# Eight more projections in the seven-product scheme, and a new filling of the attention, in a decoder layer on one core

## The reference, cut to what matters

```
u = x @ w_in ; h = h + ... swiglu (first feed-forward)
proj = u @ w_in     -> gq gk gv gr ga dq dk dv gates   (gates: 2 x 1024 columns, gr: 4 x 128)
ya = gla(gq, gk, gv, ...)                              # linear attention, 4 heads
ya = rmsnorm(ya, gla_head_norm) * silu(gr)
yb = diff_attention(dq, dk, dv, ...)                   # 4 heads, two softmax maps each
yb = rmsnorm(yb, diff_head_norm) * (1 - lam_init)
g_a, g_b = sigmoid(gates)
h = h + gate * ((g_a * (ya @ w_branch_a) + g_b * (yb @ w_branch_b)) @ w_out)
... second feed-forward, final norm
```

## Time and profile before

| what | value |
| --- | --- |
| median of 3 runs | 2144.24 us |
| the profiled execution, its own time | 2143.3 us |
| its span | 2141.5 us |
| TensorE busy | 2106.8 us, 98% of the span, 10225 matmuls |
| VectorE, ScalarE, GpSimd busy | 1354.6, 841.9, 1349.1 us |
| mean granted clock of TensorE | 0.996 |

### The profile page before, as it was taken

The page is one execution under the profiler, slowest core; times in us unless marked ns, Lnnn a source line. Parts: engine busy times, 40 slices in busy tenths (PEclk is TensorE's granted clock), DMA queues, the critical chain, the costliest instruction groups (busy, mean ns, idle before and its releaser), DMA issues.

```text
span 2141.5 us, 28194 instructions
## 1 busy us (share of the span) xinstructions
PE 2106.8 (98%) x10225; PEld 1733.8 (81%) x10225; DVE 1354.6 (63%) x2077; ACT 841.9 (39%) x1571; POOL 1349.1 (63%) x1072
## 2 busy tenths in 40 slices
PE   8999999999999999999999999999999999999998
PEld 7788778778878788888788888888788888888887
DVE  6867777778956921288666663534766444459956
ACT  7432223234445433345444452114423332234444
POOL 6688878878964677543322132336688877769943
PEclk9999999999999999999999999999999999999999
DMA  7245555558333333300111013411243333366333
GB/s 286 86 142 170 177 163 162 182 189 296 90 100 112 119 99 109 88 11 2 40 40 30 21 40 122 165 49 49 84 151 97 111 101 118 104 225 202 94 99 123
DMA packets 228618, 248.86 MB, mean 116 GB/s; under 512 B 10479, under 2 KB 155010, under 8 KB 228226
## 3 DMA queue, kind: packets, MB, share of 16 engines
q1 hardware_dynamic: 228338, 246.81, 35.7%
q10 hardware_dynamic: 144, 0.26, 0.0%
HBM read 191.98 MB, written 55.05 MB: 115 GB/s over the span
## 4 chain that ended last, share of the span: by engine, by line
PE 77%; DVE 13%; DMA 4%; issue 3%; ACT 2%; SPq 1%; POOL 0%; DVEq 0%; ACTq 0%; POOLq 0%
PE ps L2883 27%; PE ps L3038 16%; PE ps L2758 15%; PE ps L2894 6%; PE ps L2839 5%; DMA ada_half<-in_w_ada 3%; PE ps L3290 2%; PE ps L3255 1%; DVE x_op L2248 1%; DVE ada_acc L2058 1%; DMA ada_full<-in_w_ada 1%; DMA q<-in_ffn_w_out 1%; PE ps L3171 1%; PE ps L3275 1%; PE ps L3104 1%
## 5 line engine op out<-in xcount | busy, mean ns | idle before, releaser
L1213 POOL TENSOR_TENSOR w_lo<-w_raw,w_hi 128x512 fp32r<-128x512 f32 x240 | 352.2, 1478 | 91.5 <-ACT w_hi L1506 90.7
L2883 PE MATMUL ps<-t,w_hi 128*128 128x512 f32 x1280 | 396.9, 391 | 7.0 <-POOL w_lo L1213 3.4
L3038 PE MATMUL ps<-x_op,w_hi 128*128 128x512 f32 x1208 | 373.5, 390 | 4.3 <-DVE x_op L2248 3.0
L1506 ACT ACTIVATE w_hi<-w_raw 128x512 fp32r<-128x512 f32 x240 | 143.3, 624 | 381.1 <-POOL w_raw L1278 168.5
L2883 PEld LDWEIGHTS ps<-t,w_hi 128*128 128x128 f32 x1280 | 240.0, 188 | 61.3 <-DVE bufs L2271 7.0
L3038 PEld LDWEIGHTS ps<-x_op,w_hi 128*128 128x128 f32 x1208 | 226.1, 188 | 54.9 <-POOL w_lo L1213 5.7
L1213 POOL TENSOR_TENSOR w_lo<-q,w_hi 128x512 fp32r<-128x512 f32 x132 | 198.2, 1511 | 102.2 <-ACT w_hi L1506 102.2
L2883 PE MATMUL ps<-t,w_lo 128*128 128x512 f32 x640 | 249.5, 390 | 0.0
L1180 POOL TENSOR_SCALAR w_hi<-w_raw 128x1024 fp32r<-128x1024 f32 x41 | 44.4, 1084 | 323.0 <-PE ps L2758 267.8
L3038 PE MATMUL ps<-x_op,w_lo 128*128 128x512 f32 x604 | 235.1, 389 | 0.0
L2248 DVE TENSOR_TENSOR x_op<-x_raw,x_op 128x512 fp32r<-128x512 f32 x154 | 177.8, 1164 | 83.8 <-ACT x_op L1516 82.7
(11 more groups left out here) (402 smaller groups left out, 4408.0 us busy)
## 6 DMA issues: line engine op xcount, KB each, us to landing
w_raw<-in_ffn_w_in SPq DMA_DIRECT2D x88, 512.0 KB, 4.0
hid_dram<-hid_raw SPq DMA_DIRECT2D x154, 256.0 KB, 5.1
x_raw<-hid_dram SPq DMA_DIRECT2D x154, 256.0 KB, 2.6
ada_half<-in_w_ada SPq DMA_DIRECT2D x112, 256.0 KB, 2.7
w_raw<-in_w_in SPq DMA_DIRECT2D x41, 512.0 KB, 3.7
q<-in_ffn_w_out SPq DMA_DIRECT2D x6, 1536.0 KB, 9.1
ada_full<-in_w_ada SPq DMA_DIRECT2D x16, 512.0 KB, 12.3
gate_dram<-h SPq DMA_DIRECT2D x12, 512.0 KB
```

What stands on the lines that cost most here:

```text
L1213: nc.gpsimd.tensor_tensor(lo, src, hi.bitcast(F32), ALU.subtract).then_inc(hs_ready, 1)
L1506: nc.scalar.activation(hs_place(n)[0], src, ACT.Copy).then_inc(wa_high, 1)
L2883: mm = nc.tensor.matmul(ps[bank][:], w[i], x[:, k, :], start=(first and k == 0 and q == 0), stop=(k == 3 and q == 2), skip_group_check=True)
L3038: mm = nc.tensor.matmul(ps[down_bank(p) + m][:], w[:, tile(m)], x_op[:, n % 3, x, :], start=(p in (0, 1, 3) and k == 0 and q == 0), stop=( ...
```

## The change

**More in the seven-product scheme.** `GATES` grows from 12 to 20 units: all 16 gate units and the four r units (`C_GR`), so `gate_tile` runs 11 times instead of 7. For the r tiles ScalarE applies Silu instead of sigmoid. r comes back from `gate_dram` to `r_row` four times, at the start of the attention, and GpSimd multiplies `ya` by it (`gate_r`, 8 instructions). The gain of the norm moves into `norm_a` of VectorE (`scalar_tensor_tensor` for `tensor_tensor`).

**Filling by quarters.** Heads 0 to 2 have six half units (q, k, v, v, q, k) for eight steps. Each is cut in quarters of 6 matmuls and every step gets three quarters, 18 matmuls, some of them ahead of `key_scores` and some behind:

```diff
+        HALF_UNITS = [("q", 0), ("k", 0), ("v", 0), ("v", 1), ("q", 1), ("k", 1)]
+        BEFORE_SCORES = {1: (0, 3, 4), 2: (1, 2, 4), 5: (3, 3, 4), 6: (4, 2, 4)}
+        BEHIND_SCORES = {0: (0, 0, 3), 1: (1, 0, 2), 2: (2, 0, 1), 3: (2, 1, 4),
+                         4: (3, 0, 3), 5: (4, 0, 2), 6: (5, 0, 1), 7: (5, 1, 4)}
```

(step: half unit, first quarter, last quarter). In TensorE's order:

```diff
                         turn_a(hd, i)
                         if i == 1 and hd > 0:
                             turn_out(hd - 1, 1)
-                        if i == 6:
-                            fill(hd, i)
+                        if hd + 1 < DIFF_H and i in BEFORE_SCORES:
+                            fill(hd, BEFORE_SCORES[i])
...
-                        if i != 6:
-                            fill(hd, i, (lambda: turn_v_half(0, 0)) if (hd, i) == (0, 0) else None)
+                        if hd == DIFF_H - 1:
+                            filled(i)
+                        elif i != 6:
+                            fill(hd, BEHIND_SCORES[i], (lambda: turn_v_half(0, 0)) if (hd, i) == (0, 0) else None)
...
                         values(hd, i)
+                        if i == 6 and hd + 1 < DIFF_H:
+                            fill(hd, BEHIND_SCORES[i])
```

**The last head** is filled by `filled(i)`: one token half of a row of the first branch, 12 matmuls a step, four rows in all. For this the parts of `ya` must be there: ScalarE makes the high parts in head 2, step 4 and head 3, step 0 (four copies of 128x512 each, `high_ya`), GpSimd the low parts (`low_ya`, eight instructions), and GpSimd gates the eight finished pieces (`gate_row`):

```diff
+            def filled(i):
+                m, hf = filled_row(i)
+                if i == 0:
+                    pe.wait_ge(dqlo, 4 * DIFF_H)
+                else:
+                    pe.wait_ge(row_kept, i)
...
+                for k in range(4):
+                    if m == 0:
+                        pe.wait_ge(ylo_ready, 4 * hf + k + 1)
+                    mm = row_three(0, m, k, hf, ps[0])
```

**ScalarE's order.** The copy out of bank 0 is in steps 1, 2, 5 and 6 of heads 0 to 2 right behind `high_a`, in 3 and 7 behind `exps`; in the last head in every step behind `exps`:

```diff
-                        if i == 6:
+                        if hd < DIFF_H - 1 and i in BEFORE_SCORES:
                             fill_out(hd, i)
...
+                        if (hd, i) == (DIFF_H - 2, 4):
+                            high_ya(0)
+                        if (hd, i) == (DIFF_H - 1, 0):
+                            high_ya(1)
-                        if i != 6:
+                        if hd == DIFF_H - 1 or i in (3, 7):
                             fill_out(hd, i)
```

**VectorE's order.** `combine` is done one step ahead instead of two, ahead of `maxima`:

```diff
                         ahead = (hd, i + 2) if i + 2 < TT else (hd + 1, i + 2 - TT)
+                        following = (hd, i + 1) if i + 1 < TT else (hd + 1, 0)
+                        if following[0] < DIFF_H:
+                            combine(*following)
                         if ahead[0] < DIFF_H:
                             maxima(*ahead)
...
-                        if ahead[0] < DIFF_H:
-                            combine(*ahead)
```

More of the change, by code:

```diff
@@ L49 @@
 U_GA, U_GQ, U_GK, U_GV = 0, 1, 3, 5
-U_HEAD, U_BRANCH = 9, 25
-U_OUT = U_BRANCH + 12
+U_HEAD, U_BRANCH = 9, 21
+U_OUT = U_BRANCH + KT
 MIX_UNITS = U_OUT + KT
[L53 to L56, removed]
+FILLED = 4
+BRANCH_UNIT = {(br, i): U_BRANCH + 4 * br + i for br in range(2) for i in range(4)}
 MB = 0
-GATES = [(0, m) for m in range(EARLY + 1, KT)] + [(1, m) for m in range(KT)]
+GATES = [(br, m) for br in range(2) for m in range(KT)] + [(2, hd) for hd in range(GLA_H)]
+SIGMOID_TILES = KT
 GATE_TILES = len(GATES) // 2
@@ L274, in build_program, with y_part @@
         ratio = sm("ratio", [P, 2])
[L276 to L283, removed]
+        def y_part(br, part, j, hf=None):
+            if br == 0:
+                return u_hi[:, hf, 4 * part + j, :]
+            row = ((0, 1, 4, 6), (2, 3, 5, 7))[part][j]
+            if hf is None:
+                return rar[:, row * S:(row + 1) * S]
+            return rar[:, row * S + hf * HALF:row * S + (hf + 1) * HALF]
         z = [far[:, j * S:(j + 1) * S] for j in (6, 7, 5, 8, 0, 1, 2, 3)]
@@ L1840, in exps, with high_ya, high_yb @@
                                              accum_out=lsum[:, i % 2, m:m + 1]).then_inc(exp_ready, 1)
-                def high_y(br, j):
-                    copy(y_hi[br][j], (ya if br == 0 else yb)[:, j, :], yhi_ready)
+                def high_ya(hf):
+                    act.wait_ge(rt_ready, 2 * DIFF_H)
+                    for j in range(4):
+                        copy(y_part(0, 0, j, hf), ya[:, j, half(hf)], yhi_ready)
+                def high_yb(j):
+                    copy(y_part(1, 0, j), yb[:, j, :], yhi_ready)
                 def high_a(hd, i):
@@ L2613, in mixer @@
                 dve.wait_ge(bias_ready, 3)
-                for i in range(2):
-                    maxima(0, i)
-                    combine(0, i)
+                maxima(0, 0)
+                combine(0, 0)
+                maxima(0, 1)
                 for hd in range(DIFF_H):
@@ L2662, in mixer @@
                 for br in range(2):
-                    for m in range(KT):
+                    for m in range(0 if br else FILLED, KT):
                         if br == 0 and m >= 4:
-                            low_y(1, m - 4)
+                            low_yb(m - 4)
                         if (br, m) == (1, 6):
```

386 lines of the change are left out of this document (192 added, 194 removed).

## The result

| | before | after |
| --- | --- | --- |
| median | 2144.14 us (4 runs, 2140.76 to 2148.03) | **2177.07 us** (4 runs, 2173.47 to 2178.80) |
| the profiled execution, its span | 2143.3, 2141.5 | 2178.8, 2177.1 |
| mean granted clock of TensorE | 0.996 | 0.993 |

The ratio of the times is 1.0151, with a 95% interval of 1.0131 to 1.0170. The kernel became slower by 1.5%, about 33 us. The forecast was slower by 1.0%, 2165.6 us, with a range of 2135 to 2179: the direction and the range hold, and 11.5 us are missing from the sum. The time lies above the forecast's own range of 2153 to 2175, by 2 us, and inside the one that belonged to rival 3.

The account below looks back on a forecast made before the run. TensorE bounds the kernel, by a hair over the VectorE-ScalarE loop. 2143.3 - 10.9 (matmuls) + 15.9 (heads 0 to 2) + 14.4 (last head) + 2 (GpSimd) = 2164.7; median 0.9 higher: 2165.6 us, range 2135 to 2179.

Parts of the forecast that it names:

- the forecast's own range: Whole kernel: 2153 to 2175 us, for waits of 20 to 40 us in the attention; chance 0.48.
- rival 3: Attention: some nine waits over 1 us each bring 1.6 us at 1.2 GHz, +14, 2180 us; chance 0.13.
- Work by place: TensorE's matmuls: tile stage +76.2 us, attention -54.4, behind it -32.6; 48 matmuls fewer, -10.9 in all.
- The waits: Attention: TensorE waits for the VectorE and ScalarE loop, +5.3 us in each of heads 0 to 2, +14.4 in the last.
- the walk: Attention, instruction by instruction with measured durations: +5.3 us a head in heads 0 to 2; last head ends at 59.8.
- The clock, taken at 0: TensorE's clock: no drop counted in the sum, as waits stand between dense fills; 0 us.
- Head 2 was counted like the others: Attention, heads 0 to 2: the same +5.3 us for each, +15.9 for three.
- rival 3's "against": Attention: at a lower clock TensorE fills part of a wait that it would have had.
- the +2 for GpSimd: Last head: VectorE's combines slowed by 16 more GpSimd instructions, +2 us; +14 if all are hit, 0 if none.
- Rival 1: Attention: only TensorE's work counts, the loop overlaps better; faster, 2133.3 us; chance 0.24.
- rival 2: Attention: heads 0 to 2 hide their lag, only the last head waits; 2148 us, no change; chance 0.13.
- Rival 4: Tile stage: 23 us a tile, 11 x 4 us more than the sum, 2200 us; chance 0.02.

Follow-up runs that it names:

- Run 9: Changed kernel with each of ScalarE's 32 squares in the attention done twice; 2190.6 us, ratio 1.0216 to the kernel before.
- run 1: Changed kernel with VectorE's old order, combine(i+2) behind maxima(i+2); 2169.5 us, ratio 1.0103 to the kernel before.
- run 7: Run 1's kernel with the next key and query parts ahead of exps(7) and combine(7), and high_ya(0) moved to step 6 of head 2; 2163.9 us.
- run 8: Run 7's kernel, last head from step 2: ScalarE does squares, copy, next high part, then exps; VectorE combines i+1 behind maxima(i+2); 2161.7 us.
- run 11: Run 8's kernel with the second halves of the fifth and sixth half rows exchanged in the last head, copy never put off; 2154.4 us.
- run 10: Changed kernel with GpSimd's last-head work cut: 8 columns instead of 512 per gated row, 8 of 1024 in two weight splits; 2171.8 us, ratio 1.0128.
- run 6: Changed kernel with 240 extra matmuls filling all attention heads, 54.4 us of TensorE's work; 2193.0 us, ratio 1.0222 to the kernel before.

## Why the prediction was right, and where it fell short

- **Work by place.** -10.9 us in matmuls, +76.2, -54.4 and -32.6 by stage: confirmed, to 0.1 us in the tile stage and behind the attention; in the attention the work went, but not the time.
- **The range.** The forecast's own part of it, 2153 to 2175, missed. The stated range of 2135 to 2179 holds the measured 2177.1 because it took in half of rival 3. By the profiled executions 14.1 us are missing (2178.8 against 2164.7): 10.7 in the attention, 259.0 against 248.3 (270.4 - 54.4 + 32.3), and 3.8 ahead of the tile stage, less 0.3 in the linear attention.
- **The waits.** Forecast 5.3 us in each of heads 0 to 2 and 14.4 in the last; measured idle 6.2, 5.4, 6.4 and 13.6. By place they differ. Step 4 waited 0.71 for the copy (forecast 0.9), step 5 0.62 (1.3), step 6 0.59 for the key's low part and 0.72 for `low_a` (1.5 and 1.1). Two that the walk had at 0.2 or not at all made up for it: 1.45 at `turn_out` in step 1 and 1.06 for `keep_b` in step 6, which stands behind `maxima(7)` on VectorE. The sums agree, and this agreement is partly luck. Run 9 and runs 1, 7, 8 and 11 show that the mechanism is the right one.
- **The clock, taken at 0.** The reason given was "My sum has no such drop, since the waits here stand between dense fills", and it failed. Counted over the whole kernel, as the time that 128x512 matmuls took above 0.227 us where they start at the low pace, it is 10.2 us after against 4.7 before, 5.5 more. All of it is in head 2 and the last. One stretch of the last head, 1352 to 1360, had a clock of 0.57:

```profile
1352.00:1360.00 8.00, 6.18 (x18) 5.02 (x19) 2.73 (x5) 3.52 (x10) 1.28 (x1) 0.57 0.00 0
```

  In it and just ahead of it lie the idle 1.98 and 1.84 us of step 6. The Trainium skill ("TensorE: Matmul & The Clock Gate", Part 1) says that only activity keeps the array off half rate. The trace agrees, with 0.57 here. No run shows which waits draw a drop. Rival 3 was right in kind and at 14 us too high: the waits of heads 0 and 1 drew no drop. The 5.5 us are not all lost time either: by run 10 the drop of head 2, about 1.5 of them, cost nothing, as rival 3's "against" has it. In the last head no two runs separate the clock from the waits. In the filled run 6 the same count is 3.1 us.
- **Head 2 was counted like the others.** This step failed: it carries `high_ya(0)`, 2.17 us ahead of `high_a(5)` and the copy; I had only `high_ya(1)` of the last head. Its length was 2.5 above head 1's. In run 7, with `high_ya(0)` in step 6 and `combine` two ahead, heads 1 and 2 both took 60.4.
- **What a wait costs beside itself.** Heads 0 and 1 without waits would be 57.1; head 1 took 63.3 with 5.4 of idle time over 0.1 us. Some 0.8 us a head is left over, presumably in smaller gaps and in first matmuls behind a wait; the sum had nothing for it, and no run isolates it.
- **The last head.** The walk ended it at 59.8 us, and with the +2 for GpSimd at 61.8; it took 65.8. Its own work was counted as 45.4, but 66.4 before less 21.8 is 44.6. What the missing 4 us are is in part open: run 10 gained 3.8 us by taking away part of GpSimd's work, where the sum had 2 for all of it, and about 4 of the 5.5 us at the low clock lie here.
- **GpSimd beside VectorE.** +2 in the sum; run 10 measured 3.8 us in the last head for 14.5 of GpSimd's 25.0 us of work there, clock included. So this term was too small.
- **Outside the attention.** The profiled execution of after entered the tile stage 3.8 us later than that of before (754.5 against 750.8); the eleven other profiles, of kernels with the same instructions up to there, entered it at 750.3 to 753.3. So most of this is chance of one execution, and no part of the change.

As an account of what TensorE did, the attention's 259.0 is 216.0 of work (270.4 - 54.4), 31.6 of waits, about 5.5 at the low clock and 6 left over, among them the narrow matmuls at the low clock, which the count leaves out. It does not say what each would save if it were gone.

Rival 1 (the work alone counts) and rival 2 (heads 0 to 2 hide their lag) needed heads 0 to 2 at 57 us, and none of them came below 60.4 in any order tried. Rival 4's price adds up to 2209, not 2200; the tile stage, at 19.0 us a tile, rules it out either way.

## What to carry to other kernels

A stage in which TensorE is just full can have a round of the other engines that is nearly as long: before you take matmuls out of it, write down the closed round of the other engines, instruction by instruction, and keep as much of TensorE's work in the step as the round is long; here 21.8 us of products in the last head cost 2.9 us, and as much in the tile stage would cost its whole length. When a round sets the pace, an edit pays only if it takes an instruction out of the round (the high part of the next tile ahead of the exponentials) and not if it changes places inside it. A new wait among wide matmuls may also cost them their clock, here some 5.5 us beside 31.6 of waits; where the round sets the pace, the slower matmuls may only fill the next wait, as in head 2.

## What the runs showed of the hardware

- A wait of 2.70 us of PE (head 2), with dense 128x512 matmuls on both sides, was followed by matmuls 0.42 us apart for 3.7 us. The same wait in run 10 was not, nor was one of 2.78 us in the last head of the changed kernel (at 1344.11, clock 1.00 from 1344 to 1352), nor the idle 1.45 us at `turn_out` in heads 1 and 2; one of 1.69 us at `turn_out` in the last head was (clock 0.79 from 1304 to 1312). So the length of a wait alone does not tell. A mean clock of 0.993 over the whole kernel holds both.
- VectorE's `ratio`, which handles one column, took 0.22 us alone and in the rows above 0.95 and 1.13 beside instructions of GpSimd of 128x512 and 128x1024; in other places beside GpSimd it took anything from 0.22 up to 1.26 (the kernel before). The last instruction of a combine of 768 columns took 1.02 alone and 1.88 to 2.15 beside GpSimd; where GpSimd was busy for only 0.59 us of it (run 1), it still took 1.02. The maxima of 512 columns, which read from the banks, took 0.68 in both cases.
